# Projection tile 13 split among small products, four experts' weights loaded before routing, and four last token sums on TensorE

## The reference

```
h = rmsnorm(x);  proj = h @ w_in                      # 21 column tiles of 128, then 32 tiles of gates
k-norm:   kk = kk * rsqrt(max(sum_per_head(kk*kk), 1e-24))
low rank: w  = tanh(wl) @ w2,  a = sigmoid(a0 + al @ a2)
... four mixers, branch products, gates, merged @ w_out, x = x + m
h2 = rmsnorm(x)
group = argmax(h2 @ Wg + bg); the best 2 of its 4 experts; weights w_top
x = x + sum over the 2 experts of w_top * down_e(silu(gate_e(h2)) * up_e(h2))
y = rmsnorm(x)
```

## Time and profile before

| | |
|---|---|
| time, median of 3 runs | 1693.25 us (1690.97 to 1696.56) |
| the profiled execution | 1692.16 us |
| its span in the trace | 1690.3 us, 20353 instructions |
| TensorE busy | 1540.3 us |
| VectorE busy | 662.8 us |
| ScalarE busy | 349.0 us |
| mean granted TensorE clock | 0.959 of full speed |
| DMA | 192.57 MB, mean 114 GB/s |

### The profile page before, as it was taken

The page is one execution under the profiler, slowest core; times in us unless marked ns, Lnnn a source line. Parts: engine busy times, 40 slices in busy tenths (PEclk is TensorE's granted clock), DMA queues, the critical chain, the costliest instruction groups (busy, mean ns, idle before and its releaser), DMA issues.

```text
span 1690.3 us, 20353 instructions
## 1 busy us (share of the span) xinstructions
PE 1540.3 (91%) x7909; PEld 971.9 (58%) x7909; DVE 662.8 (39%) x1258; ACT 349.0 (21%) x643; POOL 200.2 (12%) x316
## 2 busy tenths in 40 slices
PE   8999799999999999999999999999999488978960
PEld 5666456667777777777777765666445332322310
DVE  5040049853353525345453432577212401101108
ACT  3110231041313131313223135000012111101102
POOL 3007300012111111110110010100000001101100
PEclk9999889999999999999999999999999789989985
DMA  6111101131412131221113121464301379776646
GB/s 199 38 38 38 29 14 38 39 112 52 112 62 58 46 116 36 72 71 34 46 51 122 34 102 46 148 239 179 137 13 63 138 300 342 252 262 228 224 162 263
DMA packets 46655, 192.57 MB, mean 114 GB/s; under 512 B 6344, under 2 KB 6840, under 8 KB 41824
## 3 DMA queue, kind: packets, MB, share of 16 engines
q1 hardware_dynamic: 27568, 114.03, 19.6%
q0 software_dynamic: 18992, 77.25, 12.6%
HBM read 344.85 MB, written 41.44 MB: 229 GB/s over the span
## 4 chain that ended last, share of the span: by engine, by line
PE 85%; DMA 5%; DVE 4%; issue 3%; ACT 2%; SPq 2%; POOL 0%; DVEq 0%; POOLq 0%; ACTq 0%
PE ps L460 37%; PE ps L824 7%; PE ps L763 7%; PE ps L886 6%; PE ps L900 4%; PE ps L707 3%; DMA arena<-in_w_gu 2%; PE ps L621 2%; PE ps L616 2%; PE ps L626 2%; PE ps L599 2%; PE ps L865 1%; SPq L393 1%; PE ps L475 1%; DVE arena L1686 1%
## 5 line engine op out<-in xcount | busy, mean ns | idle before, releaser
L460 PE MATMUL ps<-arena,wring 128*128 128x344 f32 x2208 | 668.5, 453 | 0.0
L460 PEld LDWEIGHTS ps<-arena,wring 128*128 128x128 f32 x2208 | 406.6, 190 | 191.7 <-issue 2.8
L886 PE MATMUL ps<-arena,scr 128*32 128x512 f32 x1280 | 147.7, 609 | 16.4 <-DMA arena<-in_w_gu 16.4
L1772 POOL DMA_DIRECT2D gate_scratch<-stage x96 | 52.1, 544 | 615.6 <-ACT stage L1006 542.8
L824 PE MATMUL ps<-arena 128*128 128x512 f32 x256 | 112.5, 596 | 0.0
L763 PE MATMUL ps<-arena,wring 128*128 128x344 f32 x384 | 111.2, 451 | 0.0
L886 PEld LDWEIGHTS ps<-arena,scr 128*32 128x32 f32 x1280 | 38.9, 111 | 109.8 <-issue 82.0
L763 PEld LDWEIGHTS ps<-arena,wring 128*128 128x128 f32 x384 | 72.5, 189 | 38.6
L1006 ACT ACTIVATE stage<-ps 128x344 f32<-128x344 f32 x84 | 38.4, 457 | 252.7 <-PE ps L460 252.6
L900 PE MATMUL ps<-arena,scr 128*32 128x512 f32 x640 | 76.0, 617 | 15.7 <-issue 14.2
L824 PEld LDWEIGHTS ps<-arena 128*128 128x128 f32 x256 | 47.7, 189 | 60.9 <-issue 60.0
(11 more groups left out here) (404 smaller groups left out, 1789.6 us busy)
## 6 DMA issues: line engine op xcount, KB each, us to landing
arena<-in_w_gu SPq DMA_DIRECT2D x320, 512.0 KB
arena<-in_w_dn SPq DMA_DIRECT2D x80, 1024.0 KB
wring<-in_w_all SPq DMA_DIRECT2D x61, 512.0 KB, 3.6
gate_scratch<-stage POOLq DMA_DIRECT2D x96, 172.0 KB, 2.2
arena<-gate_scratch POOLq DMA_DIRECT2D x4, 2064.0 KB, 10.2
scr<-gate_scratch POOLq DMA_DIRECT2D x4, 2064.0 KB, 10.1
arena<-y_rows SPq DMA_DIRECT2D x16, 512.0 KB, 9.6
arena<-in_w_out SPq DMA_DIRECT2D x2, 2048.0 KB, 10.2
```

Of the source, the lines that this page charges most:

```text
L460: mm = pe.matmul(ps[:, c, 0:CW], wring[:, slot, k, :], H[:, k, chunk(c)], start=k == 0, stop=k == KT - 1)
L886: mm = pe.matmul(ps[S * j:S * (j + 1), i % 2, :], XT[i % 2][:, k * P + S * j:k * P + S * (j + 1)], GU[j][:, k * 2 * HID:(k + 1) * 2 * HID] ...
L1772: pool.dma_start(gate_scratch[:, g:g + 1, chunk(c)], stage[:, c:c + 1, :]).then_inc(sem(f"gate_out{c}"), 16)
```

## The change

1. Tile 13 no longer follows the low-rank products as a whole. Its first chunk stands before the head sums, a quarter chunk (two of eight k) after each head sum and after each of the first three low-rank products, the rest after the last one. Tile 14 and `pairs(7, 10)` follow.
2. SP loads the weights of experts 0, 4, 8 and 13 (`GUESS`) for the four columns before routing is known: gate-up 0 and down 2 and 3 after the first half of the output projection, the others after its second half, ahead of the last store of normed rows. The flags of step 0 compare with the guess; SP waits until the guessed weights have landed and then issues conditional transfers as in other steps, but one whole gate-up transfer for each column. The normed rows and the router's weights lie elsewhere (`H2`, `w_r` in `scr`), since their old place is now expert weights.
3. The one-hot product is turned: `OQ` (32 columns) is stationary, `OS` (80) moving, in four column groups of the array, summed by the next small product with `eye4`; `OS` is made in two halves with a semaphore step each, so later counts of `routed` are one higher.
4. The last sum of token tiles 1, 3, 5, 7 is made on TensorE: identity times x plus two scaled identities (made by ScalarE) times the experts' rows, six float32 products of 512 columns for a tile, left in PSUM, from which ScalarE squares and VectorE norms. VectorE sums the other five tiles, in the order: sum 0, then for n = 2, 4, 6, 8 sum n, norm n-2, norm n-1, and norm 8.

```diff
 NSLOTS = (2 * T + NE * (S - 1)) // S
 STEPS = (NSLOTS + NS - 1) // NS
 ROUND = 1.5 * 2 ** 23
+GUESS = [0, 4, 8, 13]
...
@@ -371,10 +374,32 @@
             sp.wait_ge(sem("up_mm"), 12 * KT)
             sp.wait_ge(sem("wo_in"), 16)
             sp.dma_start(WO[1].rearrange("p k m -> p (k m)"), ins["w_out"][:, 1, :]).then_inc(sem("wo_in"), 16)
+            def guess_gu(j):
+
+                w = GUW // GUC
+                for h in range(GUC):
+                    sp.dma_start(GU[j][:, h * w:(h + 1) * w], ins["w_gu"][GUESS[j] * P:(GUESS[j] + 1) * P, h * w:(h + 1) * w]
+                                 ).then_inc(sem(f"gu_in{h}"), 16)
+
+            def guess_dn(j):
+
+                sp.dma_start(DN[j], ins["w_dn"][GUESS[j] * P:(GUESS[j] + 1) * P, :]).then_inc(sem("dn_in"), 16)
+
+            sp.wait_ge(sem("out_mm"), NTT)
+            guess_gu(0)
+            guess_dn(2)
+            guess_dn(3)
             for p, n in enumerate(ORD):
                 m = rows_of(n)
+                if p == NTT - 1:
+                    sp.wait_ge(sem("out_mm"), 2 * NTT)
+                    guess_gu(1)
+                    guess_gu(2)
+                    guess_dn(0)
+                    guess_dn(1)
+                    guess_gu(3)
...
@@ -405,7 +430,12 @@
             sp.wait_ge(sem("routed"), 3)
             look_up(0)
             for h in range(GUC):
-                load_gu(0, h)
+                sp.wait_ge(sem(f"gu_in{h}"), 16 * NS)
+            for j in range(NS):
+                e = sp.snap(regs[0][j], donate=False, min_val=0, max_val=NE - 1)
+                f = sp.snap(regs[0][NS + j], donate=False, min_val=0, max_val=1)
+                sp.dma_start(GU[j].unsqueeze(1), gu_e[:, bass.ds(e, 1), :], cond=f).then_inc(sem("gu_in0"), 16)
+            sp.wait_ge(sem("dn_in"), 16 * NS)
             load_dn(0)
...
@@ -499,6 +529,11 @@
             pairs(3, 6)
 
 
+            def tile13(c, lo, hi):
+
+                half(1, c, lo, hi, 6 * 6 + 3 + c - 2, 16 * 6 + 16)
+
+            tile13(0, 0, KT)
             for t in range(2):
                 pe.wait_ge(sem("lora_act"), t + 3)
                 if t == 1:
@@ -506,6 +541,7 @@
                 for c in range(NCH):
                     mm = pe.matmul(ps[:, 3 + c, 0:CW], bones, TM[:, t, chunk(c)], start=True, stop=True)
                 mm.then_inc(sem("head_sum"), 1)
+                tile13(1, 2 * t, 2 * t + 2)
 
             pe.wait_ge(sem("lora_act"), 2)
             pe.wait_ge(sem("k_ss"), 2)
@@ -517,8 +553,12 @@
                     mm = pe.matmul(ps[:, 3 + c, 0:CW], lora_w[lo:lo + 32, t * P:(t + 1) * P],
                                    PR[lo:lo + 32, S_LORA, PAD + c * CW:PAD + (c + 1) * CW], start=True, stop=True)
                 mm.then_inc(sem("lora_mm"), 1)
-
-            pairs(6, 10)
+                if n < 3:
+                    tile13(1 + n // 2, (4, 6, 0)[n], (6, 8, 2)[n])
+            tile13(2, 2, KT)
+            for c in range(NCH):
+                half(0, c, 0, KT, 6 * 6 + 6 + c - 2, 16 * 6 + 32)
+            pairs(7, 10)
...
@@ -846,13 +886,15 @@
             pe.wait_ge(sem("routed"), 2)
             pe.matmul(ps[0:1, 7, 0:NSLOTS], ECOL, ident[:, 0:NSLOTS], start=True, stop=True).then_inc(sem("slot_mm"), 1)
 
-            pe.wait_ge(sem("routed"), 4)
             for a in range(V18):
-                mm = pe.matmul(ps[0:NSLOTS, 6, 0:S], OS[:, a, :], OQ[:, a, :], start=a == 0, stop=a == V18 - 1)
+                if a % NTT == 0:
+                    pe.wait_ge(sem("routed"), 4 + a // NTT)
+                j = a % NS
+                mm = pe.matmul(ps[S * j:S * (j + 1), 6, 0:NSLOTS], OQ[:, a, :], OS[:, a, :], start=a < NS, stop=a >= V18 - NS)
             mm.then_inc(sem("slot_mm"), 1)
-            pe.wait_ge(sem("routed"), 5)
+            pe.wait_ge(sem("routed"), 6)
             for j in range(NS):
-                pe.matmul(ps[S * j:S * (j + 1), 4, 0:STEPS], SLT[0:NSLOTS, :], ident[0:NSLOTS, STEPS * j:STEPS * (j + 1)],
+                pe.matmul(ps[S * j:S * (j + 1), 4, 0:STEPS], cc("eye4"), SLT[:, STEPS * j:STEPS * (j + 1)],
...
@@ -881,7 +923,7 @@
                     pe.wait_ge(sem("act"), i - 1)
                 for k in range(KT):
                     if k % (KT // GUC) == 0:
-                        pe.wait_ge(sem(f"gu_in{k * GUC // KT}"), 16 * NS * (i + 1))
+                        pe.wait_ge(sem(f"gu_in{k * GUC // KT}"), 16 * NS * (i + (1 if k * GUC // KT else 2)))
...
@@ -912,6 +954,19 @@
                 if i + 1 < STEPS:
                     gate_up(i + 1)
                 down(i)
+
+            pe.wait_ge(sem("diag"), 2 * len(ON_PE))
+            for b, n in enumerate(ON_PE):
+                if b == 0:
+                    pe.wait_ge(sem("yo_ev0"), STEPS)
+                    pe.wait_ge(sem("yo_ev1"), STEPS)
+                pe.wait_ge(sem(f"rows_in{n}"), 32 + (16 if n < len(X_PARTS) else 0))
+                for h in range(2):
+                    half_ = slice(h * HALF, (h + 1) * HALF)
+                    pe.matmul(ps[:, 2 * b + h, :], ident, X2[:, n, half_], start=True, stop=False)
+                    for c in range(2):
+                        mm = pe.matmul(ps[:, 2 * b + h, :], DIAG[:, b, c, :], YG[n][c][:, half_], start=False, stop=c == 1)
+                mm.then_inc(sem("tail_mm"), 1)
...
@@ -1190,11 +1245,18 @@
                 if i + 1 < STEPS:
                     gated(i + 1)
                 downed(i)
+            act.wait_ge(sem("xt_mm"), STEPS)
+            for b, n in enumerate(ON_PE):
+                for c in range(2):
+                    A(DIAG[:, b, c, :], ident, ACT.Copy, scale=q1[5 + c][:, n:n + 1]).then_inc(sem("diag"), 1)
             for n in range(NTT):
                 m = rows_of(n)
-                act.wait_ge(sem("comb"), n + 1)
+                if n in ON_PE:
+                    act.wait_ge(sem("tail_mm"), ON_PE.index(n) + 1)
+                else:
+                    act.wait_ge(sem("comb"), n // 2 + 1)
                 act.wait_ge(sem("row_sq"), NTT + n)
-                A(STG[0:m, 0:D], X2[0:m, n, :], ACT.Square, accum_out=SS[0:m, n:n + 1]).then_inc(sem("row_sq"), 1)
+                A(STG[0:m, 0:D], XSUM[ON_PE.index(n)] if n in ON_PE else X2[0:m, n, :], ACT.Square, accum_out=SS[0:m, n:n + 1]).then_inc(sem("row_sq"), 1)
...
-            def norm_row(n, count, dst, gain, sem_name, free):
+            def norm_row(n, count, dst, gain, sem_name, free, src=None):
...
                     dve.wait_ge(sem(name), value)
-                stt(dst[0:m, :], X2[0:m, n, :], rs, GAIN[0:m, gain, :], MUL, MUL).then_inc(sem(sem_name), 1)
+                stt(dst[0:m, :], X2[0:m, n, :] if src is None else src, rs, GAIN[0:m, gain, :], MUL, MUL).then_inc(sem(sem_name), 1)
...
@@ -1633,6 +1695,7 @@
             dve.wait_ge(sem("slot_mm"), 2)
             link(ts(EID[0:1, :], ps[0:1, 7, 0:NSLOTS], float(NE - 1), None, MIN))
             e3, c3 = (a_[0:1, :].rearrange("p (j i) -> p j i", j=NS) for a_ in (EID, CHG))
+            link(tt(c3[:, :, 0], e3[:, :, 0], cc("guess")[0:1, :], ALU.not_equal))
...
@@ -1645,9 +1708,11 @@
             link(stt(ROW, SLOT, -float(S), POS, MUL, ADD))
             link(tt(OQ, last(ROW, S), mid(cc("count", 0, S), V18), EQ))
             link(tt(OQ, OQ, last(cc("tokv"), S), MUL))
-            tt(OS, last(SLOT, NSLOTS), mid(cc("count", 0, NSLOTS), V18), EQ).then_inc(sem("routed"), 1)
+            for c in range(2):
+                tt(OS[:, c * NTT:(c + 1) * NTT, :], last(SLOT[:, c * NTT:(c + 1) * NTT], NSLOTS), mid(cc("count", 0, NSLOTS), NTT), EQ
+                   ).then_inc(sem("routed"), 1)
             dve.wait_ge(sem("slot_mm"), 3)
-            nc.vector.tensor_copy(SLT[0:NSLOTS, :], ps[0:NSLOTS, 6, 0:S]).then_inc(sem("routed"), 1)
+            nc.vector.tensor_copy(SLT, ps[:, 6, 0:NSLOTS]).then_inc(sem("routed"), 1)
...
@@ -1678,19 +1743,25 @@
                     dve.wait_ge(sem(f"yo_out{i % 2}"), 16 * (i // 2))
                 nc.vector.tensor_copy(YO[i % 2][:, HALF:D], ps[:, 6, :]).then_inc(sem("yo_ev1"), 1)
 
-            for n in range(NTT):
+            def combined(n):
+
                 m = rows_of(n)
-                for c in range(2):
-                    dve.wait_ge(sem(f"rows_in{n}"), 32 + (16 if n < len(X_PARTS) else 0))
-                    r_ = X2[0:m, n, :]
-                    ins_ = stt(r_, YG[n][c][0:m, :], q1[5 + c][0:m, n:n + 1], r_, MUL, ADD)
-                    if c == 0:
-                        link(ins_)
-                    else:
-                        ins_.then_inc(sem("comb"), 1)
-                if n:
-                    norm_row(n - 1, NTT + n, YB[(n - 1) % 3], 1, "y_ready", [(f"y_out{(n - 1) % 3}", 16 * ((n - 1) // 3))] if n >= 4 else [])
-            norm_row(NTT - 1, 2 * NTT, YB[(NTT - 1) % 3], 1, "y_ready", [(f"y_out{(NTT - 1) % 3}", 16 * ((NTT - 1) // 3))])
+                dve.wait_ge(sem(f"rows_in{n}"), 32 + (16 if n < len(X_PARTS) else 0))
+                r_ = X2[0:m, n, :]
+                link(stt(r_, YG[n][0][0:m, :], q1[5][0:m, n:n + 1], r_, MUL, ADD))
```

(13 more changed lines are left out.)

36 lines of the change are left out of this document (19 added, 17 removed).

## The result

| | before | changed |
|---|---|---|
| time, median | 1693.17 us (4 runs, 1690.97 to 1696.56) | 1678.53 us (4 runs, 1676.40 to 1680.95) |
| ratio | | 0.9898, 95% interval 0.9881 to 0.9916 |
| the profiled execution | 1692.16 us, span 1690.3 | 1680.95 us, span 1679.1 |
| mean granted TensorE clock in it | 0.959 | 0.973 |

Faster, and inside the range; the gain is 14.6 us where 21.3 were forecast. The profiled execution of the changed kernel is the slowest of its four. The page of the changed kernel, beside the earlier trace rows: TensorE is busy 16 us longer, with the sums that VectorE gave up, in a span 11 us shorter.

A forecast was written before the change was run, and what follows sets the result against it. TensorE, busy 91% of the span and carrying 85% of the chain, was taken as the bound. Gains 12.1 + 4.2 + 5.0 = 21.3 us gave 1672.0 us against the median of 1693.25; range 1664.5 to 1682.

The forecast's parts named there:

- the forecast's own case: Whole kernel: the summed gains hold, gain 15 to 24 us, time 1669 to 1678; chance 0.68.
- rival 3: Pieces partly cold, or gather as slow as before because the reload fills its time: gain 6 to 15 us; chance 0.13.
- Part 1: Low-rank products: tile 13 in pieces fills TensorE's idle time, so tile 14 starts earlier; gain 12.1 us.
- VectorE "keeps about 3.1": Before the last projection's copy: of VectorE's 6.05 us of slack about 3.1 remain.
- Routing 3.1: Routing: one-hot in halves and cheaper turned matmuls save net 3.1 us, bounds 1.0 to 3.8.
- Gather, 7.7 to 6.6: First gather of 128 rows: engines carry only column 2's reload, so it gains 1.1 us.
- The bound of -1: First gather: lower end of its forecast gain, whose bounds were -1 to 2.7 us.
- Loads ahead of the last store of normed rows: Before routing: 14 loads (8.4 MB) queue ahead on SP; store lands by 1340, before the gather, costing nothing.
- Part 3, 5.0: End of kernel: last sums of tiles 1, 3, 5, 7 on TensorE gain 5.0 us, bounds 2 and 7.9.
- until about 20 us after the first sum: End of kernel: a sign to look for, tile 3's norm waiting that long for the first store.
- the slower case: TensorE's clock stays low in the pieces and last sums, time 1707 us; chance 0.03 slower.
- the mild one: First store does not hold the last stretch, or restart is mild: gain 24 to 29 us; chance 0.12.

The follow-up runs named there:

- part 1 alone: The kernel before with only tile 13 in pieces among the head sums and low-rank products; 1687.65 us, ratio 0.9958.
- kernel with early copies: The changed kernel with ScalarE copying tile 13's first two chunks out among the sigmoids, before the inverse roots; 1668.71 us, ratio 0.9856.
- the fastest one: The changed kernel with guess 9 for column 2, tile 13's first two chunks copied early and six y buffers together; 1665.68 us, ratio 0.9823.
- part 2 alone: The kernel before with only the guessed expert loads and the turned one-hot product in halves; 1691.10 us, ratio 0.9977.
- second profile: The changed kernel, nothing altered, run and profiled once more beside follow-up kernels; 1678.38 us, ratio 0.9918.
- Six buffers: The changed kernel with six buffers for y instead of three, so norms 3 to 5 wait for no store; 1676.36 us, ratio 0.9901.

## Why the prediction was right or wrong

Direction and range were right, the size was 6.7 us too large: 14.6 lies just under the forecast's own case (15 to 24, chance 0.68) and at the upper end of rival 3's (6 to 15, chance 0.13). Point by point:

- **Part 1, 12.1 at tile 14: right in size and mechanism.** With the clock at 1.00, sigmoids 3.29 apart (3.2 said), the last beginning at 215.40 (214.9 with the offset), TensorE idle for 7.39 (7.5) until ScalarE's copy, tile 14 at 226.42 (225.9 with the offset). Scans 11.2 + 1.0 = 12.2 earlier. The fall to half clock behind the idle piece was foreseen, and cost about 2.
- **That the gain of part 1 reaches the end: wrong, and unsaid in the sum.** Every later stage was taken as keeping its length, and the opening too, which gave the offset of 1.0. In the profile 1.7 and 1.6 us went in two stretches partly at 1.2 GHz (5.30 and 6.46 us instead of 3.62 and 4.90), and part 1 alone gave 6.3 in the median. Who pays this I can list, not explain. Of the nine profiled executions whose scans begin between 358.9 and 361.1, seven have the first place slow (5.20 to 5.66) and two not (3.62, with scans at 359.59 and 359.64); all nine have the second slow (6.38 to 7.95). The kernel with early copies pays neither, the fastest one both, and part 2 alone pays the second (7.66) although its edits all lie later. So the edit of part 1 is not its only cause, and what else decides is open. One thing goes with it: the two whose first place is fast are the two of the nine whose opening 48 products took least (15.67 and 15.71 us, the others 15.86 to 16.92).
- **VectorE "keeps about 3.1": the number is nearly right (2.63), the reading wrong.** It was one of two waits; with the 5.19 behind it VectorE had 7.8. This cost nothing in the prediction, but it hid the best next step, which gave 9.7 in the median.
- **Routing 3.1: right in mechanism, 3.7 in size**, 32.9 to 29.2 us from output projection to gather, with the 36 instructions at 1.83 us.
- **Gather, 7.7 to 6.6: wrong, and the sign too.** It went to 9.7 (9.4 in the second profile). The text took "the engines will carry only column 2's reload" as a lighter load and so a faster gather. What counts is not how much is queued: the first packet starts 4.2 to 4.4 us after the issue with 3 MB in front as with 5, and then the gather shares packet by packet, now with packets of 8 KB instead of 4. The three kernels with no load ahead (4.3 to 4.5), the four with step 0's weights as before (7.7 to 8.0) and the seven with the reload just ahead (9.1 to 9.7) agree. The bound of -1, from the spread of the 20 gathers, is half of what it lost. By the Trainium skill (DMA: Bandwidth & Descriptors, Queues, rings and completion order) the engines take turns between queue rows, a packet at a time. The packets of the traces agree, 186 against 192 and 144 against 143; the estimate of 2.5 us beside weights that I had made from it lacks the time before the first packet, 4.2 of the 7.7 us, and the estimate of 1.3 alone lacks 1.7 of the 4.3.
- **Loads ahead of the last store of normed rows: no cost**, as said. That store landed 18.0 us after its issue instead of 2.6, and the gather still waited only for its index.
- **Part 3, 5.0: right mechanism, 3.7 in size.** Sum by sum: TensorE needs 5.15 us a tile and starts at half clock (2.05 for two instructions that later take 1.02); tile 1's norm waits 1.53 for ScalarE's square; norm 3 meets the store. The term that was off is "until about 20 us after the first sum": 21.4 to 21.9 in all kernels with the new sums and three buffers on SP's queue, 20.1 to 20.5 in those without. Six buffers give back 2.9, which confirms the wait. Part of the store's 11.7 us is SP's queue (6.9 from ScalarE's). By the Trainium skill (the same page and section) descriptors of a ring are consumed in order on each DMA engine; the two runs agree, with the store 1.6 us behind tile 7's rows on SP's queue and 2.8 ahead of them on ScalarE's. The 1.3 is that these rows are late themselves, with the instruction packet as the candidate; the first store's later issue (9.6 us after the first sum instead of 7.0) comes when all rows loads are already issued in both kernels.
- **Expert steps keep their length: not in one execution.** 268.7 us instead of 267.2, 266.0 in the second profile of the same kernel, 264.3 to 271.7 over the study.

The account of the two profiled executions, by the table of leads: 11.2 (part 1 less the offset) - 2.9 (the two slow places, 3.2, less 0.3 elsewhere) + 3.7 (routing) - 2.0 (gather) - 0.8 (first product, clock) - 1.5 (steps) - 0.1 + 3.7 (end) = 11.3, the 11.2 between the spans within rounding. The second profile of the changed kernel (span 1674.6, a lead of 15.7) has 11.2 - 3.0 + 3.7 - 1.6 + 0.7 (first product) + 1.1 (steps) + 0.2 + 3.5. So what the forecast lacks in both is the offset of 1.0, about 3 at the two places, about 3 at the gather (1.1 said, -1.6 to -2.0 found) and 1.3 to 1.5 at the end, against 0.6 more from routing; first product and steps went one way in one and the other way in the other.

Of the rivals, rival 3 named the reload as what holds the gather back and had the measured time at its edge; its other condition, partly cold pieces, did not come, and the loss at the two later places stands in no rival. That the time fell inside the range is in part luck for this reason. Neither the slower case nor the mild one showed. One slip of the sum: the bounds of part 2's two terms add to 0 to 6.5, where the text has 0.5 to 6.5 and the range takes 1.5 and 6.2; the range is hardly changed by it.

## To carry over

For a transfer on a latency path, fewer bytes in flight is no price: count the time to its first packet with engines free or busy (1.7 or 4.2 us here) and then the packet sizes of whatever shares the engines with it. Before naming an engine as the next bound, add up all its waits in the stretch, not the first. And a step that a trace confirms to a tenth can still lose half of itself later, at the places where TensorE idles for a few us and starts again: forecast those as a bound below.

## What the hardware did that was not expected

- **The spread between executions goes with TensorE's clock.** Over 115 executions of these kernels, each against the mean of its own kernel in its group, span and mean granted clock go together with a correlation of -0.81, 1.14 us for each 0.001 of clock. The six of the kernel with early copies run from 1663.62 us at 0.979 to 1675.82 at 0.971. Which is the cause is not shown, as the clock is also at 0.50 where TensorE waits. A change of 3 us in one place is smaller than this.
- **The same idle piece is followed by full clock in one kernel and by half in another**: after sixteen instructions of 8 columns, 1.17 us of idleness and eight small products, 3.62 to 5.66 us for the same 16 instructions; after 3.34 us of idleness 4.89 to 7.95.
- **The opening differs as well**: the first 48 products took 15.67 to 16.92 us in the fourteen profiles, and all that follows is shifted by it.
- **A gather of 128 rows (0.52 MB) took 4.3 to 4.5 us without other loads, 7.7 to 8.0 beside weight packets of 4 KB, 9.1 to 9.7 beside those of 8 KB**, with its first packet 1.7 us after the issue in the first case and 4.2 to 4.4 in the others.
- **The same store took 11.7 us from SP's queue behind its loads and 6.9 from ScalarE's.**
- **One packet of 16 KB of instructions takes 1.0 us of a DMA engine**, in the midst of the rows loads of every kernel with the new sums.
